# Work at three seams moved into the neighbouring product, one gate pass summed in PSUM, and a top-k decode in 16-bit pairs

## The reference

```python
h = h + (g_a * y_a + g_b * y_b) @ w_mix_out[l]
```

```python
qh = (xt @ peer_w_q).reshape(T, PEER_HEADS, 2, PEER_HALF)
sub = jnp.einsum("thpc,hpnc->thpn", qh, peer_sub_keys)
v1, i1 = lax.top_k(sub[:, :, 0], PEER_TOPK)
v2, i2 = lax.top_k(sub[:, :, 1], PEER_TOPK)
cand = (v1[..., :, None] + v2[..., None, :]).reshape(T, PEER_HEADS, PEER_TOPK * PEER_TOPK)
vals, cidx = lax.top_k(cand, PEER_TOPK)
e1 = jnp.take_along_axis(i1, cidx // PEER_TOPK, axis=-1)
e2 = jnp.take_along_axis(i2, cidx % PEER_TOPK, axis=-1)
...
a = jax.nn.gelu(h, approximate=False) * gc
return jnp.einsum("chk,chkd->cd", a, v_sel)
```

## Time and profile before

| what | us |
|---|---|
| three runs | 3390.03, 3388.58, 3387.81 (median 3388.58) |
| the profiled execution | 3388.43 |
| its span, first to last instruction | 3386.6 |
| PE busy in the span | 3269.3 (97%) |
| DVE busy | 2289.1 (68%) |
| ACT busy | 1547.5 (46%) |

### The profile page before, as it was taken

How to read it: one execution, slowest core, us unless ns; L and a number is a source line. 1 busy time by engine, 2 the same in 40 slices (tenths; PEclk the granted TensorE clock), 3 DMA queues, 4 the chain that set the end, 5 groups by cost and what they waited for, 6 DMA issues and landing times.

```text
span 3386.6 us, 51716 instructions
## 1 busy us (share of the span) xinstructions
PE 3269.3 (97%) x20430; PEld 2881.2 (85%) x20430; DVE 2289.1 (68%) x3238; ACT 1547.5 (46%) x1954; POOL 5.6 (0%) x14
## 2 busy tenths in 40 slices
PE   8999999999999999998899999899999999999999
PEld 6999998788888888886689988888888888888887
DVE  5654455676576566697659999568778577865554
ACT  4554434555355355445544443443444443435353
POOL 0000000000000000000000000000000000000000
PEclk9999999999999999999999999999999999999999
DMA  6545665565656665551355554564555655566665
GB/s 231 158 149 194 199 192 174 176 198 189 193 185 187 198 187 183 164 169 60 112 163 161 164 167 137 156 182 148 181 179 182 187 187 178 182 186 187 193 187 167
DMA packets 161247, 590.43 MB, mean 174 GB/s; under 512 B 17904, under 2 KB 18064, under 8 KB 159728
## 3 DMA queue, kind: packets, MB, share of 16 engines
q1 hardware_dynamic: 160192, 583.14, 55.6%
q0 software_dynamic: 816, 3.98, 0.3%
HBM read 584.96 MB, written 2.10 MB: 173 GB/s over the span
## 4 chain that ended last, share of the span: by engine, by line
PE 86%; DVE 10%; ACT 2%; issue 1%; DMA 0%; DVEq 0%; SPq 0%; ACTq 0%
PE PS L407 19%; PE PS L366 12%; PE PS L368 12%; PE PS L367 12%; PE PS L410 9%; PE PS L376 6%; PE PS L377 6%; PE PS L378 6%; DVE LO L292 3%; PE PS L1346 1%; DVE GB L982 1%; PE PS L1335 1%; PE PS L591 0%; PE PS L662 0%; ACT UN L618 0%
## 5 line engine op out<-in xcount | busy, mean ns | idle before, releaser
L292 DVE TENSOR_TENSOR LO<-RAW,HI 128x1024 fp32r<-128x1024 f32 x1096 | 1327.7, 1218 | 826.6 <-ACT HI L291 824.9
L291 ACT ACTIVATE HI<-RAW 128x1024 fp32r<-128x1024 f32 x1096 | 1150.7, 1055 | 1287.1 <-PE PS L368 627.5
L407 PE MATMUL PS<-XX,HI 128*128 128x512 f32 x2688 | 736.4, 395 | 0.0
L376 PE MATMUL PS<-XX,HI 128*128 128x256 f32 x2176 | 624.4, 287 | 11.8 <-DVE LO L292 7.8
L377 PE MATMUL PS<-XX,HI 128*128 128x256 f32 x2176 | 616.7, 283 | 0.0
L378 PE MATMUL PS<-XX,LO 128*128 128x256 f32 x2176 | 616.4, 283 | 0.0
L366 PE MATMUL PS<-HI,FH 128*128 128x512 f32 x1504 | 595.0, 396 | 14.1 <-DVE FL L533 9.6
L368 PE MATMUL PS<-HI,FL 128*128 128x512 f32 x1504 | 588.0, 391 | 0.0
L367 PE MATMUL PS<-LO,FH 128*128 128x512 f32 x1504 | 586.8, 390 | 0.0
L407 PEld LDWEIGHTS PS<-XX,HI 128*128 128x128 f32 x2688 | 460.1, 189 | 61.9
L410 PEld LDWEIGHTS PS<-XX,LO 128*128 128x128 f32 x2688 | 412.5, 189 | 57.3
(11 more groups left out here) (251 smaller groups left out, 2348.3 us busy)
## 6 DMA issues: line engine op xcount, KB each, us to landing
RAW<-in_peer_v SPq DMA_DIRECT2D x256, 512.0 KB, 3.9
RAW<-in_ffn_w_up SPq DMA_DIRECT2D x176, 512.0 KB, 4.1
RAW<-in_peer_ut_rest SPq DMA_DIRECT2D x160, 512.0 KB, 3.9
RAW<-in_w_in SPq DMA_DIRECT2D x136, 512.0 KB, 3.9
RAW<-in_peer_ut SPq DMA_DIRECT2D x96, 512.0 KB, 3.6
RAW<-in_ffn_w_down SPq DMA_DIRECT2D x88, 512.0 KB, 3.8
RAW<-in_w_mix_out SPq DMA_DIRECT2D x32, 512.0 KB, 4.2
RAW<-in_w_in_2c SPq DMA_DIRECT2D x32, 512.0 KB, 4.2
```

What stands on the lines that cost most here:

```text
L291: hi_done.append(AC.do(lambda e, raw=raw, hi=hi: e.activation(hi, raw, ACT.Copy), landed[i], used))
L292: lo_done.append(DV.do(lambda e, raw=raw, hi=hi, lo=lo: e.tensor_tensor(lo, raw, hi.bitcast(F32), ALU.subtract), hi_done[i], landed[i], used))
L376: e.matmul(o, h, x, start=f, stop=False, skip_group_check=True)
L407: e.matmul(o, hi[:, k, w], XX[:, 4 * u + k, :, :].rearrange("p h s -> p (h s)"), start=u == 0 and k == 0, stop=False, skip_group_check=True)
```

## The change

1. `mixed`: the splits of quarters 0 to 2 at the first seam become an evacuation that runs beside the last product of the second branch; the split of quarter 3 stays behind it.
2. `against_keys`: the key scores at the second seam become an evacuation that runs after the first unit of the next product (for the fourth group, of the first `up_staged` product).
3. `choose` decodes in 16-bit pairs: key numbers are written twice each as bf16, a bf16 list 0 to 15 is made, compare and multiply run on bf16 with an innermost pair, and the multiplication is cut into its two heads.
4. `gates(0, 1)` sums the three parts in PSUM as r = 1 does.
5. `first_blocks`: the third seam's gate multiplications become a background generator behind `first_gates`; a quarter can begin as soon as the third block's product for it has been put down, which for quarter 3 is the last product.

```diff
+    def mixed(js, m_read):
+        for j in js:
+            mix_ready[j] = split(XH[:, 4 * j:4 * j + 4, :], XL[:, 4 * j:4 * j + 4, :], GA[:, 4 * j:4 * j + 4, :],
+                                 m_read, m_yb[j])
+            yield
...
         if g == 3:
             m_x_read = m
+            evacuations.append(mixed(range(0, 3), m))
...
-        if g == 3:
-            for j in range(4):
-                mix_ready[j] = split(XH[:, 4 * j:4 * j + 4, :], XL[:, 4 * j:4 * j + 4, :],
-                                     GA[:, 4 * j:4 * j + 4, :], m_x_read, m_yb[j])
+    advance([mixed(range(3, 4), m_x_read)])
...
-        m = DV.do(lambda e: e.tensor_copy(f16, i16), m_i)
+        m = [DV.do(lambda e: e.tensor_copy(twice, i16.unsqueeze(2).to_broadcast([128, 64, 2])), m_i),
+             DV.do(lambda e: e.tensor_copy(first16, const("iota")[:, 0:16].unsqueeze(2).to_broadcast([128, 16, 2])),
+                   m_i)]
...
-            m1 = DV.do(lambda e, w=w, io=io, c3=c3: e.tensor_tensor(c3, io, w, ALU.is_equal), m1)
-            m1 = DV.do(lambda e, p=p: e.tensor_tensor(CANE[:], CANE[:], f4[:, :, p, :].unsqueeze(2).to_broadcast(
-                [128, 2, 16, 16]), ALU.mult), m1, m)
-            m1 = DV.do(lambda e, p=p, c3=c3: e.tensor_reduce(halves[p], c3, AX.X, ALU.add), m1)
+            m1 = DV.do(lambda e, c4=c4: e.tensor_tensor(
+                c4, first16.unsqueeze(1).to_broadcast([128, 16, 16, 2]),
+                which.rearrange("p (q j) -> p q j", j=2).unsqueeze(2).to_broadcast([128, 16, 16, 2]), ALU.is_equal),
+                m1, m)
+            c5 = c4.rearrange("p (h q) m j -> p h q m j", h=2)
+            m1 = [DV.do(lambda e, p=p, c5=c5, h=h: e.tensor_tensor(
+                c5[:, h], c5[:, h], f5[:, h, p].unsqueeze(1).to_broadcast([128, 8, 16, 2]), ALU.mult), m1)
+                for h in range(2)]
+            m1 = DV.do(lambda e, p=p, c4=c4: e.tensor_reduce(
+                halves[p].rearrange("p (q j) -> p q j", j=2), c4.rearrange("p q m j -> p q j m"), AX.X, ALU.add), m1)
...
+    def against_keys(g, qh, m_qh):
+        for t in range(2):
...
+            m = PE.do(fn, fr, m_qh, m_keys)
...
+        m_keys_read.append(m)
+        yield
...
-        if g < 3:
-            background.extend(choose(t, g) for t in range(2))
-    m_keys_read = m
-    background.extend(choose(t, 3) for t in range(2))
+        evacuations.append(against_keys(g, qh, m_qh))
+        background.extend(choose(t, g) for t in range(2))
...
-        apart = r != 1
+        apart = r > 1
...
+    def first_blocks():
+        nonlocal hb_free
+        for j in range(4):
+            while len(staged[2]) <= j:
+                yield
+            m_first[j] = DV.do(lambda e, j=j: e.tensor_tensor(blocks(GM[2], j), blocks(GM[2], j), blocks(GM[0], j),
+                                                         ALU.mult), staged[0][j], gm_ready[0])
+            m_moved[j] = AC.do(lambda e, j=j: e.activation(blocks(GM[0], j), blocks(UF, j), ACT.Copy), m_first[j],
+                               staged[2][j])
+            yield
+            hb_free = weighted(1, j, [staged[1][j], hb_free], blocks(STAGE, j), HB[:], [m_moved[j]] * 8)
+            ready[1].append(hb_free)
+            yield
...
-    background.append(first_gates())
+    background.extend([first_gates(), first_blocks()])
```

More of the change, by code:

```diff
@@ L176, in _program @@
     CAND = GB[:].rearrange("p (h i k) -> p h i k", i=16, k=16)
-    CANE = over("CANE", [128, 2, 16, 16], 32 * K)
+    CANE = over("CANE", [128, 16, 16, 2], 32 * K, BF16)
     assert arena + 40 * K <= 229344, arena
@@ L1189, in choose @@
         vals, cidx, sel = W[:, 192:224], W[:, 224:256].bitcast(U32), W[:, 256:288].bitcast(U32)
-        self_, sm = W[:, 288:320], W[:, 352:354]
-        f4 = f16.rearrange("p (h s k) -> p h s k", s=2, k=16)
+        which, sm = W[:, 288:304].bitcast(BF16), W[:, 352:354]
+        first16 = W[:, 320:336].bitcast(BF16).rearrange("p (m j) -> p m j", j=2)
+        twice = f16.bitcast(BF16).rearrange("p (x j) -> p x j", j=2)
+        f5 = twice.rearrange("p (h s k) j -> p h s k j", s=2, k=16)
         before = last_choice[0]
@@ L1214, in choose @@
             m1 = DV.do(lambda e, op=op, n=n: e.tensor_scalar(sel, cidx, n, None, op), ms, m1)
[L1215 to L1218, removed]
-            m1 = DV.do(lambda e, w=w, io=io, c3=c3: e.tensor_tensor(c3, io, w, ALU.is_equal), m1)
-            m1 = DV.do(lambda e, p=p: e.tensor_tensor(CANE[:], CANE[:], f4[:, :, p, :].unsqueeze(2).to_broadcast(
-                [128, 2, 16, 16]), ALU.mult), m1, m)
-            m1 = DV.do(lambda e, p=p, c3=c3: e.tensor_reduce(halves[p], c3, AX.X, ALU.add), m1)
+            m1 = DV.do(lambda e: e.tensor_copy(which, sel), m1)
+            c4 = CANE[:]
+            m1 = DV.do(lambda e, c4=c4: e.tensor_tensor(
[8 more added lines that the diff above has]
+                halves[p].rearrange("p (q j) -> p q j", j=2), c4.rearrange("p q m j -> p q j m"), AX.X, ALU.add), m1)
             yield
@@ L1235, in _program, with fn @@
     qh_free = [None, None]
[L1236 to L1242, removed]
+    m_keys_read = []
+    def against_keys(g, qh, m_qh):
         for t in range(2):
             i, b, fr = spare()
-            def fn(e, g=g, t=t, b=b, qh=qh):
+            def fn(e, t=t, b=b):
                 for j in range(4):
@@ L1257, in _program @@
             m_sub[t].append(t_free[i])
-        if g < 3:
-            background.extend(choose(t, g) for t in range(2))
-    m_keys_read = m
-    background.extend(choose(t, 3) for t in range(2))
+        m_keys_read.append(m)
+        yield
+    rate[0] = 0.9
+    for g in range(4):
+        pair, banks, m = product(False, 16, XH, XL, x_ready)
+        qh = QH[g % 2]
+        acc_free[pair] = m_qh = [AC.do(lambda e, i=i, qh=qh, b=banks[i]: e.activation(
+            qh[:, 2 * i:2 * i + 2, :], two(b), ACT.Copy), m, qh_free[g % 2], box2["pt_read"], conv_ready)
+            for i in range(2)]
+        evacuations.append(against_keys(g, qh, m_qh))
+        background.extend(choose(t, g) for t in range(2))
     m_tab = []
@@ L1436, in first_gates, with blocks @@
         yield from gates(0, 1)
+    def blocks(a, j):
+        return a[:, 4 * j:4 * j + 4, :]
+    m_first, m_third, m_moved = [None] * 4, [None] * 4, [None] * 4
+    def first_blocks():
[11 more added lines that the diff above has]
+            yield
     ready = [[] for _ in range(8)]
     staged = [[] for _ in range(3)]
-    background.append(first_gates())
+    background.extend([first_gates(), first_blocks()])
     up_staged(GM[2], staged[0], m_keys_read)
@@ L1444, in _program @@
     flush()
[L1446 to L1456, removed]
     def multiply_third():
```

## The result

The changed kernel takes 3361.08 us (median of 6 runs, 3357.78 to 3362.28) against 3388.82 us for the kernel before beside it (6 runs, 3387.42 to 3390.06). The ratio is 0.9917, 95% interval 0.9904 to 0.993. Forecast were 3357.0 us and a range of 3350 to 3370. The profiled execution of after takes 3359.69 us (span 3357.9, granted clock 0.993), 28.7 us less than that of before, where the sum said 31.7.

What follows compares the result with a forecast made beforehand. DVE was taken to set the pace in the choices and first gates, an ACT-DVE-PE chain at the seams. Gains 6.6 + 13.4 + 8.3 (second seam and decode) + 3.4 = 31.7 us off 3388.43 gave 3357 us, range 3350 to 3370.

Steps and rivals of the forecast that it cites:

- First seam: Splits moved beside the second branch's last product remove a 3.94 us wait and a lower-clock first unit: gain 6.6 us.
- Third seam: Before `down`, only quarter 3 stays behind the last product, so two waits and lower-clock stretches go: gain 13.4 us.
- that rival: At the third seam, quarter 3's chain exceeds 8.2 us and the fourth unit waits about 4.2 us: 3363 us, chance 0.12.
- up to 2 us late, against three units of cover: Beside the last `up_staged` products, ACT's move waits for DVE's multiplication, delaying the next HI; prepared units were to cover it.
- Second seam: At query copies and choices, DVE's first max starts 1.4 us earlier and its waits for HI shrink by 3.2 us.
- Decode: In the choices, 16-bit pairs save 0.47 us a choice over eight choices: 3.7 us.
- -0.37 for a lookup: In the decode, compare saves 0.27 us and the halved multiplication 0.1, for each of two lookups a choice.
- +0.27 for the list 0 to 15 and the doubled key numbers: In the decode, preparing these operands adds 0.27 us to each choice.
- The rival of pairs that don't pack: In the decode, DVE loses 5.2 us instead of gaining 3.7: 3366 us, chance 0.08.
- Gates: First gate pass: without reductions four waits go, each block costs PE 0.71 us, 103.2 becomes 99.8 us: gain 3.4.
- The rival of waits that stay: In the first gates, builds still come late and PE also pays 9.0 us more: 3369 us, chance 0.1.
- the slower rival: From 1850 to 2005 us, short PE waits lower the clock, 2.3 us a unit; 20 units give 3403 us, chance 0.02.

Runs made afterwards that it cites:

- run 6: Changed kernel with a blank step behind each moved step of the third seam's generator; 3353.73 us in one run.
- run 3: Changed kernel with the key scores put back at the second seam, ahead of the next product; 3367.24 us.
- run 7: Changed kernel with gate passes r = 2 and r = 3 summed in PSUM too; 3377.36 us.
- run 5: Changed kernel with the first gate pass again side by side in PSUM with DVE's reductions; 3365.44 us.
- run 10: Changed kernel with blank steps in the third seam's generator and rates 0.75 and 1.25 instead of 0.9 and 1.15; 3362.2 us, ratio 0.9914.
- run 1: Changed kernel with all four splits of the first seam put back behind the second branch's last product; 3366.05 us.

## Why the prediction was right, and where it was not

**First seam: right.** 6.6 us said; 6.58 between the two profiles, 6.54 by undoing it. Wait and clock were both in the sum, and quarter 3's split was ready in time.

**Third seam: right at the seam, wrong ahead of it.** The seam gave 13.36 of 13.4. Quarter 3's chain, from the eviction at 2152.87 on, met three prepared units, and that rival falls. The step that failed is "up to 2 us late, against three units of cover". The lateness of a single step was sized about right: 4.43 us in a unit of 2.88 is 1.55. But it was set once against a cover of 8.6 us, while it recurs in every unit that has a step, and is 5.04 us where two fall into one. Three HI intervals ran up 9.8 us; 3.25 of it stands in the first, which is as long in run 6 and does no harm there. The runs show it from both sides: with the steps taken out, or with a blank step behind each, the stretch is 44.09 us, and 47.77 with them. Of the 3.95 us lost against before, 3.7 are this; the rest, 43.82 to 44.09, is not (the dearer matmuls of the last block, 0.77 for 0.52 us, lie there). That the total still came out near the sum is in part luck: this loss was partly made up by the next two terms.

**Second seam: right in its size, and its mechanism fits.** Start 1.4 said, 1.56 measured. Waits of DVE 3.2 said; behind the start they fell from 4.5 us (9.8 less 5.3) to 1.6, which is 2.9. Undoing the move costs 4.1 beyond the start, but the two edits of this stretch overlap: undone alone they cost 5.66 and 4.89, 10.55 together, and in one they gave 9.76. The worth of PE's four waits apart from DVE's was not shown, since run 3 brings back both.

**Decode: a term too small.** 3.7 us said, 4.89 by undoing it. The compare (425 ns for a forecast 418), the halves (289 for 285) and the reduction (687, as its float32 kind) were right. So is -0.37 for a lookup: from start to start the two lookups fell by 0.40 and 0.39. What failed is the term "+0.27 for the list 0 to 15 and the doubled key numbers". The two copies, 221 and 175 ns where one of 188 stood, make the choice's line only 0.12 us longer from start to start. A start-to-start reading of neighbouring small DVE instructions would have given the better price. The rival of pairs that don't pack falls with the halves' 289 ns. The figure worked out from the Trainium skill's "VectorE: DVE Perf Modes" (an estimated 194 ns for a half) is off by 95 ns here; the row of before was the better guide. The same section also says that this formula under-predicts and gives a measured fixed term of about 150 cycles; with it a half is an estimated (150 + 128) / 0.96 = 290 ns, and the trace's 289 agrees.

**Gates: right.** 99.8 us said, 99.65 measured; a block costs PE 0.71 us on the mean. The rival of waits that stay falls: of 9.0 us in four, 0.6 is left in one. The price for PE is confirmed where nothing offsets it, in run 7.

**The clock: the slower rival did not come.** PEclk is 1.00 in the choices although PE has ten waits, 6.1 us in all, none over 1.0 us, and 1.00 in the window with the waits of 1.72 and 1.52. It falls to the lower level behind the waits of 3.94, 4.62 and 4.20 of the kernel before (0.66 from 2188 to 2193 us, behind the last). The section of the Trainium skill named in the prediction, on short idles that make the clock swing ("TensorE: Matmul & The Clock Gate"), has no case in the choices. In the first gates of run 5 it may have one: there the clock fell behind two of four waits between groups of matmuls, those of 2.07 and 2.62 us.

So the profiled execution lies 3.0 us above the 3356.7 of the sum: 3.95 lost in the fourth stretch and 0.6 outside the stretches, less 1.5 that the second seam with the choices gained beyond its term and 0.2 from the gates; the two other seams fell short by 0.06 together. The median is 1.4 us above that execution.

## What to carry to other kernels

Work that is moved beside a product and passes from one in-order engine to another and back makes the product's own preparation wait too. Price it by the chain in one unit against the unit's time, and count it for as many units in a row as carry a step: lateness adds up, and the cover is used up once. Spacing the steps is worth trying too: here it gave back the 3.7 us that the moved steps of the third seam had cost, but what is spaced too far falls back to the seam, where run 10 lost 10.2 us.

## What the runs showed of the hardware

The granted clock did not follow the length of a wait alone. Waits of 1.72 and 1.52 us left it at 1.00, and so did one of 3.04 us in run 10 (its window from 2145 to 2157 us). In the first gates of run 5 it fell to the lower level behind waits of 2.07 and 2.62 us (0.83 from 2009 to 2019 us, 0.66 from 2086 to 2096), but not behind those of 1.42 and 2.77 (1.00 from 2036 to 2046 and from 2062 to 2072). A wait of 3.94 us in run 1 was followed by matmuls 0.43 us apart instead of 0.23 for 5.2 us, and behind the 7.44 us of run 10 the clock is 0.72 from 2161.7 to 2167. What else decides was not tried.

DVE's sum over 512 bf16 elements takes 687 ns, no less than over float32 (686), while the compare in pairs takes 425 against 692 and each half of the multiplication 289. So the narrower type helped the elementwise part of the decode and not its reduction.
